# Folding rotation, forget gates and modulation rows into neighbouring stages, and finishing three projections tile by tile, in a two-block fp32 transformer kernel

## The reference

```python
# first block
mod = silu(c) @ w_ada + b_ada                       # 6 rows of 1024: shift, scale, gate, twice
h = rmsnorm(x) * (1 + sc1) + sh1                    # the context likewise
q, k, v, ff, fb, hv, hq, hg = split(h @ w_in)       # the context without q, hq, hg
q, k = rope(q), rope(k)                             # the context's keys aren't rotated
lam = exp(sum(q1*k1)) - exp(sum(q2*k2)) + lambda_init
a = softmax(q_1 k_1) - lam * softmax(q_2 k_2)
f = lb + (1 - lb) * sigmoid(ff or fb); k_hg = 1 - f # recurrence in both directions, log f as decay
x = x + gt1 * rmsnorm(concat(a v, recurrence * silu(hg)) @ w_out)
h = rmsnorm(x) * (1 + sc2) + sh2
x = x + gt2 * rmsnorm(expert_choice_ffn(h))         # 16 experts, router logits from h
# second block
x = x + gated_deltanet(rmsnorm(x))                  # ends in @ gdn_w_out
x = x + square(relu(rmsnorm(x) @ mlp_w1)) @ mlp_w2
return rmsnorm(x)
```

## Time and profile before

| | |
|---|---|
| median of 3 executions | 1975.47 us (1972.47 to 1976.48) |
| profiled execution | 1974.1 us |
| its span, first to last instruction | 1972.3 us |
| mean granted clock of PE | 0.935 |
| instructions | 25862 |
| PE busy | 1767.3 us, 90% |
| DVE busy | 760.8 us, 39% |
| ACT busy | 511.1 us, 26% |
| POOL busy | 134.2 us, 7% |
| HBM read | 314.34 MB, 162 GB/s over the span |

### The profile page before, as it was taken

One profiled execution on the slowest core, in us unless ns is written; L12 is line 12 of the kernel. 1 busy time (PEld: TensorE's weight loads), 2 busy tenths in 40 slices (PEclk: granted clock), 3 DMA queues, 4 the chain that ended last, 5 costly groups with the idle time before them and its releaser, 6 DMA issues. The chain is left out here.

```text
span 1972.3 us, 25862 instructions
## 1 busy us (share of the span) xinstructions
PE 1767.3 (90%) x11218; PEld 1264.6 (64%) x11218; DVE 760.8 (39%) x1072; ACT 511.1 (26%) x861; POOL 134.2 (7%) x111
## 2 busy tenths in 40 slices
PE   4999997978794999999999499998896989999997
PEld 2788873758644543444443388887896458888886
DVE  1412125749525122222222577615547143333333
ACT  2312132840211101111110433224243143223231
POOL 0000001000000000000000012103421001101010
PEclk8999997976896999999999799978998999999999
DMA  9121225030107899999999622200000332232201
GB/s 360 44 86 43 86 100 244 1 129 2 45 0 299 334 431 430 429 429 430 429 430 430 234 86 86 85 1 1 4 4 1 128 139 86 97 117 85 86 1 43
DMA packets 60545, 320.20 MB, mean 162 GB/s; under 512 B 5952, under 2 KB 6288, under 8 KB 45712
## 3 DMA queue, kind: packets, MB, share of 16 engines
q1 hardware_dynamic: 60432, 318.55, 40.3%
HBM read 314.34 MB, written 4.19 MB: 162 GB/s over the span
## 5 line engine op out<-in xcount | busy, mean ns | idle before, releaser
L1452 PE MATMUL bank<-ring,xinT 128*64 128x512 f32 x592 | 131.5, 594 | 1.7 <-ACT slot_affinity L1525 1.7
L2461 DVE TENSOR_TENSOR mlp_w_lo<-ring,mlp_w_hi 128x1024 fp32r<-128x1024 f32 x64 | 77.9, 1220 | 82.2 <-ACT mlp_w_hi L2415 82.2
L552 DVE TENSOR_TENSOR in_w_lo<-ring,in_w_hi 128x1024 fp32r<-128x1024 f32 x32 | 39.2, 1225 | 175.1 <-ACT in_w_hi L526 175.1
L250 PE MATMUL bank<-h4T_hi,mlp_w_hi 128*128 128x512 f32 x256 | 100.3, 392 | 4.1 <-DVE h4T_lo L2466 4.1
L250 PE MATMUL bank<-mlp_w_hi,up_hi 128*128 128x512 f32 x256 | 100.0, 391 | 3.5 <-DVE x L2479 3.5
L250 PE MATMUL bank<-h4T_hi,mlp_w_lo 128*128 128x512 f32 x256 | 100.3, 392 | 0.0
L250 PE MATMUL bank<-h4T_lo,mlp_w_hi 128*128 128x512 f32 x256 | 100.1, 391 | 0.0
L250 PE MATMUL bank<-mlp_w_hi,up_lo 128*128 128x512 f32 x256 | 99.7, 389 | 0.0
L250 PE MATMUL bank<-mlp_w_lo,up_hi 128*128 128x512 f32 x256 | 99.6, 389 | 0.0
L2415 ACT ACTIVATE mlp_w_hi<-ring 128x1024 fp32r<-128x1024 f32 x64 | 67.4, 1055 | 121.8 <-PE bank L250 121.0
L1452 PE MATMUL bank<-expert_slab,xinT 128*64 128x512 f32 x432 | 95.9, 593 | 0.0
(11 more groups left out here) (402 smaller groups left out, 3626.4 us busy)
## 6 DMA issues: line engine op xcount, KB each, us to landing
ring<-w_gate SPq DMA_DIRECT2D x19, 2048.0 KB, 21.0
ring<-w_up SPq DMA_DIRECT2D x18, 2048.0 KB, 21.0
ring<-w_down SPq DMA_DIRECT2D x17, 2048.0 KB, 19.8
ring<-mlp_w SPq DMA_DIRECT2D x16, 2048.0 KB, 8.4
expert_slab<-w_down SPq DMA_DIRECT2D x15, 2048.0 KB, 21.2
expert_slab<-w_up SPq DMA_DIRECT2D x14, 2048.0 KB, 20.0
expert_slab<-w_gate SPq DMA_DIRECT2D x13, 2048.0 KB, 19.4
ring<-w_ada SPq DMA_DIRECT2D x12, 2048.0 KB, 13.3
```

The lines of the kernel that those rows point to most:

```text
L250: mm = pe.matmul(out, x, y, start=(start and i == 0), stop=(stop and i == 2))
L552: dve.tensor_tensor(lo, slab_part(m, s, i, by_rows), hi, ALU.subtract).then_inc(w_lo, 1)
L1452: mm = pe.matmul(bank[half * H:(half + 1) * H, b, :], xin[:, 4 * r + k, (e % 2) * H:(e % 2 + 1) * H], expert_slab(m, s)[:, k, half * COLS: ...
L2461: dve.tensor_tensor(lo, slab_part(m, s, i, n is not None), hi, ALU.subtract).then_inc(w_lo, 1)
```

## The change

1. modulation turns its rows into columns by four transposes in place of 16 small products.
2. rotary is gone: its three steps for a unit follow that unit's product in project_in; its banks are 6 and 7, and the units have six. The lambda vectors are loaded there.
3. forget_gates is gone: the sigmoid and the bounds of f are made as project_in copies the banks out; the keys 1 - f are made by ACT in attention, one head and direction at every second step; the eight slabs of `w_ada` are multiplied in recurrence between its levels, through two slots, into banks 6 and 7, with bias and norm weights added as rows by DVE; columns and gates come at the end of mix_outputs.
4. residual, turn_ffn, turn_gdn and turn_mlp are gone. project_out, scatter and gdn_project_out run both norms, the transposes and the next operand's split tile by tile (`norm_steps`, `split_steps`), the squares over halves of a tile. project_out makes the router's logits too. scatter adds the sum of the other experts by a product with the identity, and it and gdn_project_out make the first four quarters of the next stage (`AHEAD`) on tokens 0 to 255; gdn_project and mlp begin with the same quarters on tokens 256 to 511.
5. Slabs from S_IN to S_OUT use slots 0 and 1. RELEASE is (mix_outputs, gdn_project, gdn_scan).

```diff
@@ project_in
+    UB = 6
...
+            def rotate(u):
+
+                r = turns.index(u)
+                pe.wait_ge(*emptied(u))
+                if r >= 2:
+                    pe.wait_ge(by_sin, r - 1)
+                pe.matmul(bank[:, UB + r % 2, :], m.rot, turn_of(u), start=True, stop=True).then_inc(turned, 1)
+
...
-                    if u >= 8 and not (by_rows and i):
-
-                        pe.wait_ge((act_out, dve_out)[u % 2], u // 2 - 3)
+                    if u >= UB and not (by_rows and i):
+
+                        pe.wait_ge(*emptied(u - UB))
...
+                    if u - 1 in turns and not (by_rows and i):
+                        rotate(u - 1)
...
+                pool.wait_ge(turned, r + 1)
+                pool.tensor_tensor(turn_of(u), turn_of(u), m.cos, ALU.mult).then_inc(by_cos, 1)
...
+                        act.activation(dst, bank[:, u % UB, 0:n], ACT.Sigmoid if kinds[u] == "forget" else ACT.Copy).then_inc(act_out, 1)
...
+                dve.tensor_tensor(tmp[:, r % 2, :], bank[:, UB + r % 2, :], m.sin, ALU.mult).then_inc(by_sin, 1)
+                dve.wait_ge(by_sin, r + 1)
+                dve.wait_ge(by_cos, r + 1)
+                dve.tensor_tensor(x, x, tmp[:, r % 2, :], ALU.add)
...
+                        dve.tensor_scalar(dst, dst, rest_lb[:, j:j + 1], lb[:, j:j + 1], ALU.mult, ALU.add)
@@ attention
+                if n % 2 == 0 and 0 <= n < 2 * 2 * HEADS:
+                    d, h = divmod(n // 2, HEADS)
+                    act.activation(m.kl[d][:, h, :], z[d][:, h, :], ACT.Identity, bias=m.ones[:, 0:1], scale=-1.0)
@@ recurrence
+            stream(sp, m, I, S_REST + 2, S_EXP, lambda s: (rest_done, s - S_REST + 1))
...
+                if l == cross - 1:
+                    dve.wait_ge(rest_done, 8)
+                    dve.wait_ge(bias_in, 12 * 16)
+                    dve.tensor_tensor(m.rest_rows[:, :, :], bank[:, 6:8, :], bias[:, :, :], ALU.add).then_inc(bias_added, 1)
+                    dve.wait_ge(bias_added, 1)
+                    dve.tensor_tensor(m.rest_rows[:, :, :], m.rest_rows[:, :, :], norm[:, :, :], ALU.mult).then_inc(bias_added, 1)
...
+                if l < cross - 1:
+                    if l == 0:
+                        pe.wait_ge(diag_out, 1)
+                    for j in ((0,), (1,), (2, 3), (4, 5), (6, 7))[l]:
+                        slab_wait(pe, m, S_REST + j)
+                        ada_rows(pe, m, 6, m.ring[:, slot_of(S_REST + j)].rearrange("p a b -> p (a b)"), 8, j, 0, 7).then_inc(rest_done, 1)
@@ mix_outputs
+            for g in range(4):
+                mm = pe.matmul(bank[:, TT + g, :], sel[:, g, :], m.rest_rows[:, g // 2, :], start=True, stop=True)
+            mm.then_inc(gates_ready, 1)
+            pe.wait_ge(gates_out, 1)
+            for b in range(2):
+                for j in range(4):
+                    mm = pe.transpose(bank[:, TT + b, j * P:(j + 1) * P],
+                                      m.rest_rows[:, b, :].rearrange("p (q j) -> p j q", j=4)[:, j, :], m.ident)
@@ project_out, on PE
+                    mm.then_inc(n.ready, 1)
+                    if t and half == 0:
+                        n.turn(pe, t - 1)
+                if t:
+                    logits(t - 1)
+            n.turn(pe, TT - 1)
+            logits(TT - 1)
@@ scatter, on PE
+                    pe.matmul(bank[:, 2 * t + half, :], m.ident, m.moe[:, t, cols], start=True, stop=False)
...
+            n.turn(pe, 0)
+            n.turn(pe, 1)
+            start(0)
+            n.turn(pe, 2)
+            start(1)
+            start(2)
+            n.turn(pe, 3)
+            start(3)
@@ gdn_project, on PE (mlp likewise)
+            for q in range(AHEAD):
+                ahead_product(pe, m, q, [shaped(b, False) for b in m.gdn_ahead[q]], h, late).then_inc(used, 1)
```

More of the change, by code:

```diff
@@ L462, in project_in @@
             quarters.append((S_IN + s, i, not major, made))
+        kinds += ["forget" if name in ("zf", "zb") else "gate" if name == "hg" else "plain"] * (len(units) - len(kinds))
     NQ = len(quarters)
+    turns = [u for s in range(2) for q in quarters[4 * s:4 * s + 4] for u in q[3][:1]]
     h_hi, h_lo = m.sem("h_hi_ready"), m.sem("h_lo_ready")
@@ L483, in used, with by_act, by_dve, emptied @@
         return part_done, sum(not completes(j) for j in range(q + 1))
+    def by_act(u):
+        return kinds[u] == "forget" or (kinds[u] == "plain" and u % 2 == 0)
+    def by_dve(u):
+        return kinds[u] == "plain" and u % 2 == 1
+    def emptied(u):
+        if by_act(u):
+            return act_out, sum(by_act(v) for v in range(u + 1))
+        return dve_out, sum(by_dve(v) for v in range(u + 1))
+    def turn_of(u):
+        return units[u][2]
     with nc.Block() as block:
@@ L1214, in _, with logits @@
         def _(sp):
-            loads(sp, ready)
+            sp.dma_start(m.x[:, :, :], I["x"][0].rearrange("(t p) d -> p t d", p=P)).then_inc(x_in, 16)
+            sp.dma_start(m.w_router[:, :, :].rearrange("p (r j) e -> p r j e", r=2), I["w_router"][0].rearrange("(r p j) e -> p r j e", r=2, j=4)).then_inc(m.router_in, 16)
+            stream(sp, m, I, S_EXP + 3, S_EXP + SLOTS)
+            stream(sp, m, I, S_EXP, S_EXP + 1, lambda s: (n.ready, 2 * TT))
         @block.tensor
         def _(pe):
-            products(pe, ready)
+            def logits(t):
+                pe.wait_ge(h_act, t + 1)
+                pe.wait_ge(h_dve, t + 1)
+                if t == 0:
+                    pe.wait_ge(m.router_in, 16)
+                for k in range(KD):
+                    pe.matmul(bank[:, 0, t * EXPERTS:(t + 1) * EXPERTS], m.h2T[:, k, t * P:(t + 1) * P], m.w_router[:, k, :],
+                              start=(k == 0), stop=(k == KD - 1))
@@ L1300, in turn_ffn, with take @@
-def turn_ffn(nc, m, I):
-    turn_features(nc, m, "h2T", [rows_of(m.xn2, k) for k in range(KD)], m.h2T, m.a2[:, :], m.mod[:, 16:24, 0],
-                  loads=lambda sp: stream(sp, m, I, S_EXP, S_EXP + 2))
+            def take(t):
+                dve.wait_ge(n.turned, 2 * t + 2)
+                for k in range(4, KD):
+                    ins = dve.tensor_scalar(m.h2T[:, k, t * P:(t + 1) * P], bank[:, 2 * t + 1, (k - 4) * P:(k - 3) * P],
+                                            m.a2[:, k:k + 1], m.mod[:, 16 + k, 0:1], ALU.mult, ALU.add)
+                ins.then_inc(h_dve, 1)
@@ L1605, in scatter @@
 def scatter(nc, m, I):
+    bank, x, xn = m.bank, m.x, m.xn3
     last = EXPERTS // 2 - 1
-    def products(pe, ready):
-        for t in range(TT):
-            for n in range(2):
-                for part in range(2):
-                    mm = pe.matmul(m.bank[:, 2 * t + n, :], m.spread[:, last % 2, t * P:(t + 1) * P],
-                                   m.y[part][:, n * COLS:(n + 1) * COLS], start=(part == 0), stop=(part == 1))
-            mm.then_inc(ready, 1)
-    residual(nc, m, I, "out2", m.x, m.xn3, products, lambda sp, ready: None, None, m.gate2, m.moe)
```

757 lines of the change are left out of this document (423 added, 334 removed).

## The result

The changed kernel takes 1943.07 us (median of four, 1941.65 to 1953.29) against 1975.26 before; the ratio is 0.985, with a 95% interval of 0.982 to 0.988. That is 32.2 us less. Forecast were 40.7 less, about 1935; the measured median is 8 us above that and inside the range of 1916 to 1955. The profiled execution has a span of 1940.0 us against 1972.3.

The account below looks back on a forecast made before the run. PE, busy 90% of the span, was taken to bound the kernel, so time falls only where PE idles or its work goes. Terms summed to -40.7 us from 1974.1: 1933.4 profiled, about 1935 as a median, range 1916 to 1955.

Parts of the forecast that it names:

- Stages gone: Rotary and forget-gate stages: their whole stretches go, -27.5 and -26.3 us, with their pieces priced elsewhere.
- Projection, +19.6: Input projection: eight rotation products on PE, +6.9 us, and six pauses of PE waiting for banks, +12.7.
- R2: Projection: each new pause is followed by 25 us at half PE clock, 54 us lost, 1989; chance 0.03.
- R3: Projection: eight POOL products each hold DVE up for their whole length, 10.2 us, 1945; chance 0.10; forecast took 0.
- Recurrence, +9.3: Recurrence: PE and DVE late for slabs by 2 x 3.4 us, plus 2.5 for two DVE additions.
- at two levels, the fourth and fifth: Recurrence: a slot's round of 10.5 us against DVE's 7.1 makes PE late by 3.4 at each.
- R1: Recurrence: slab loads take 13.3 us, late by 8.0 at three levels, 26.5 instead of 9.3, 1952; chance 0.12.
- Attention, +4: Attention: ACT makes eight key pieces of 0.72 us, 5.7 in all, partly in idle time; ends 0 and 5.7.
- Scatter, -9.2: Scatter to first deltanet quarters: tile 3's chain, followed through three engines' lists, ends the stage at 38.6 us with hand-over.
- Out-projections: First out-projection to router logits, -3.6 us; second out-projection to fourth MLP quarter, -5.5, from tile-by-tile work and half products.
- R4: Both out-projections and scatter: finishing tile by tile gives nothing, terms -3.6, -9.2, -5.5 go, 1953; chance 0.13.
- Mix stage, +2.6: Mix stage: selecting products 3.4 us, copy 1.0, transposes 1.6, of which the norm's tail hides about 3.4.

Follow-up runs that it names:

- copies-first kernel: Changed kernel, but in the projection ACT and DVE empty all of a quarter's banks but the last before splitting the quarter after next; 1927.24 us, ratio 0.976.
- rows spread: Changed kernel with modulation slabs' rows at other recurrence levels: two behind level 0, one each behind 1 to 4, two behind 5; 1932.19 us, ratio 0.978.
- the one pair of executions with equal clock: Changed kernel with attention's keys made by POOL instead of ACT (1941.43 us), against the copies-first kernel: attention 86.3 against 90.4 us.

## Why the prediction was right, and where it was not

The time was in the range and the sign and the main terms held, but the sum was nearer than its parts: four terms were too favourable by 13.3 us together (recurrence 7.3, scatter 2.8, projection 1.8, second out-projection 1.4), the others too unfavourable by 4.8 net. That they offset each other in part is chance.

*Stages gone.* Rotary and the forget gates gave 27.5 and 26.2 of 27.5 and 26.3. A stage that is gone gives its whole length by definition; what could go wrong was the price of its pieces in their new places, which has terms of its own.

*Projection, +19.6 against +21.4.* The pauses were read off two rows and the order of ACT's list, 12.7 against 11.8, and the copies-first kernel shows that this order, on ACT and DVE, is the whole cause. The first was longer, as forecast (3.16 against 3.2). Missing was the clock: from the first pause's start to the second's are 13.99 us, from there to the third's 11.15, while the first pause is only 1.47 longer; the other 1.4 us are the drop, out of the 2.7 by which the term exceeds rotations and pauses. Rival R2 had the right mechanism at a price that is far off: a drop costs 1.4 to 2.7 us, not 12.5, and it comes behind one of the six pauses, not all.

*Port, R3.* The collision is there. DVE's sums of keys took 1.70 us in three of four cases in the changed kernel beside POOL's product of 1.30, and 0.69 for the queries; and POOL's product beside a split, which also reads two tiles, stretched it from 1.23 to 2.12 us at three query quarters. In the copies-first kernel no sum meets a product any more, but seven splits do:

```profile
105.42 1.70 DVE L599 TENSOR_TENSOR kT<-kT,rot_sin 128x512 f32<-128x512 f32 x1
73.11 2.13 DVE L590 TENSOR_TENSOR in_w_lo<-ring,in_w_hi 128x1024 fp32r<-128x1024 f32 x1 [3.03 <-ACT in_w_hi L557]
...
99.72 2.13 DVE L593 TENSOR_TENSOR in_w_lo<-ring,in_w_hi 128x1024 fp32r<-128x1024 f32 x1 [4.10 <-ACT in_w_hi L557]
```

(The first two rows are of the changed kernel, the third of the copies-first kernel.) DVE was idle for 2.9 to 9.8 us ahead of each split or of the split before each sum, and none of PE's six pauses ends with one of these instructions. Price 0 was right, and the projection of 243.2 us, with all eight products and seven collisions in it, shows it. The Trainium skill, page "SBUF — State Buffer", section "Who interferes with whom", states the exclusion, and the rows agree with it. Whether keys made by POOL would hold up DVE's sums in attention by the same rule was not tested. While POOL worked (313.86 to 320.26) DVE had only reductions of a bank and instructions on one or two columns, and its first instruction with two wide inputs came at 322.60.

*Recurrence, +9.3 against +16.6.* The mechanism, a slot's round against DVE's pace, was right; the step that failed is its size, "at two levels, the fourth and fifth" with a round of 10.5 us. Three things were missing. The first pair was taken to be in time, but slab 3's slot is freed only by slab 1's rows (they end at 422.5), slab 3 is wanted behind slab 2's at 428.2, and lands at 431.4. The load was 8.6 us in the median and not 8.3, and 9.8 for the last slab (its slot free at 444.7, its rows from 454.5), which is loaded beside the one before it. And behind the waits for slabs PE's clock was low, so that rows counted at 1.77 took 2.81 and 3.64. The round was 11.4 to 11.7 us, and DVE was late by 13.1 us at three levels instead of 6.8 at two. R1 had the right number of levels, for the wrong reason (a load of 13.3). The run with rows spread shows that neither loads nor PE's work were short: the order alone cost 11.5 us.

*Attention, +4 against +2.4.* The price was right in the one pair of executions with equal clock, 4.1; over all it is 2 to 4.

*Scatter, -9.2 against -6.4.* The step that failed is the chain "followed": it took the norm weights as landed. The load is issued 15.4 us before it lands, behind a slab. With it early, the term is -12.0 in one execution and -8.9 in the other (217.1 and 220.1 against 229.0). The stage with its hand-over was put at 38.6 us; it took 41.2 with the wait, and 36.1 and 36.4 without. So apart from the wait the chain was put some 2 us too long, and this error hid a part of the other.

*Out-projections.* -3.6 and -5.5 against -4.6 and -4.1. In the second, products and three turns were put at 55.2 + 4.7 us and took 63.2; the difference is the stop of 4.08 us ahead of the first turn, which the sum didn't have, with the lower clock behind it, less what the turns took under 4.7. R4, that finishing tile by tile gives nothing, is wrong for the whole: the three terms gave 15.1 of 18.3 us. At the scatter and the second out-projection the early halves give this gain.

*Mix stage, +2.6 against +0.6.* Its own time grew by 1.7; the following transposes were 1.1 us shorter. Neither is more than scatter: in the other executions of the same code the stage took 18.6 to 21.5 us, and the transposes 4.8 us at a granted clock of 1.00 or 6.5 at 0.74.

## What to carry to other kernels

When work is folded from a stage of its own into a bounded one, the cost is seldom in the instructions but in where the in-order engines put the copy that frees a bank or the use that frees a slot: look for what each release stands behind, and put releases ahead of preparations for later. The same holds for a norm that stands behind splits which wait for a load. A cyclic pair of slots is paced by the round from use to next use, not by the load; use each slab as soon as it has landed, one per step, rather than pairs. Small loads that a norm needs should be issued ahead of the last big ones, since here one landed behind them, after 15.4 us.

## What the runs showed that I had not expected

POOL's scale-and-shift of 128x768 takes 0.81 us (3.22 for four), while its product of two 128x512 operands takes 1.27 to 1.30: 1.05 against 2.5 ns a column. I had estimated 1.9 from the other.

In the projection, pauses of 1.69 and 1.78 us left PE's clock at 2.4 GHz, and pauses of 3.16, 3.87, 4.16 and 5.33 us were each followed by 3.0 to 5.4 us at 1.2 GHz, at a cost of 1.4 to 2.7 us. A long pause isn't needed for a drop: in the changed kernel's recurrence PE paused for only 1.18 and 0.75 us between small score products, and the granted clock was 0.50 from 415.5 to 419.1, where the same products took 3.63 us instead of 2.06.

Between executions of the same code attention took 90.4 to 93.8 us at granted clocks of 0.92 to 0.87. So the same stage can differ by 3 us between executions, and a gain of a few microseconds is read more safely from the stage that was edited than from the kernel's median.
